# Two fixed expert pairs loaded ahead, the router by token, and the shared expert in turns 2 and 8

## Chip, cores and metric

The kernel runs on one core of a Trainium2 chip. The metric is device time in microseconds (us) of one launch, as the median of several runs. The granted TensorE clock of a row is a share of full speed: 1.00 is 2.4 GHz, 0.50 is 1.2 GHz.

## The reference

256 tokens of width 1024 go through two transformer blocks. The first block ends in a mixture of experts, and that is where the change lies:

```
h2 = modulate(rms_norm(x, norm2_g), shift2, scale2)
y  = moe_ffn(h2, w_router, router_bias, w_gate_e, w_up_e, w_down_e, w_gate_sh, w_up_sh, w_down_sh)
x  = rms_norm(x + gate2 * y, final_g)

def moe_ffn(xt, ...):                      # xt: 256 tokens x 1024
    scores = sigmoid(xt @ w_router)        # 64 experts
    choice = scores + router_bias          # best groups of 8, then the 8 best experts of a token
    wts    = scores of the 8 chosen, normed to a sum of 2.5
    routed = sum over chosen experts of swiglu(xt, gate_e, up_e, down_e) * wts
    return routed + swiglu(xt, w_gate_sh, w_up_sh, w_down_sh)

swiglu(x, g, u, d) = (silu(x @ g) * (x @ u)) @ d      # inner width 256
```

The second block begins with a gated feed-forward part (FF1, inner width 2816), whose first norm uses `ffn1_pre_g_2`. Attention and a second feed-forward part follow. All data are fp32.

## The kernel before

The program is written engine by engine, with semaphores between the engines. Each engine works off its own instructions in the order in which they stand. SP issues nearly all loads, also in order: a wait in SP's queue holds back every load behind it.

Dense products are kept exact by splitting both operands into a high and a low part (fp32r) and doing three matmuls. ACT makes the high parts (`split_hi`, `transposed`), DVE the low parts (`split_lo`), TensorE (`pe`) multiplies. Expert products are plain fp32 matmuls on the raw weights.

The weights of the dense parts live in `raw_g`, `raw_d`, `g_hi`, `g_lo`, `d_hi` and `d_lo`. The expert stage lays its `ring` over the same memory: two slots, each for one pair of experts (gate, up and down of both, six transfers of 1024 KB).

**Routing.** After the second output projection (groups `G_WO`, `G_WO+1`) DVE writes the normed rows to `h` and counts `h_ready`. Then TensorE transposes `h` for all 256 tokens, ACT and DVE split the transposed rows and the router's weights, and TensorE computes scores with experts on partitions (L2557, L2560). They are turned back and DVE picks the experts of each token in `route(b)` (L1672 to L1693), b being the block of 128 tokens. TensorE then counts the rows of each expert and ranks them (L2572 to L2579), DVE sets small and big flags (L1700 to L1705), TensorE sums them up (L2586 to L2589), and DVE computes the place of each expert in the order of turns (L1713 to L1723). TensorE applies the places (L2593 to L2595), and DVE writes `order_i` (L1733), on which SP waits (`ordered`) to load experts by their place.

The shared expert is one step of the dense machinery (`G_SH`, `D_SH`). Its gate/up stands on TensorE between the scores and the ranks, its down part on both sides of the last routing step.

**Turns.** 64 experts are worked off in 28 turns, `KINDS = "PPQPPBPPQPPPBPPQPPBPPPPBPPPQ"`. P is a plain turn of two experts with up to 64 rows each, Q a quad turn of four experts with up to 32 rows (it takes two pairs, so both slots of the ring), B one big and one small expert. Each turn consists of: gate/up of its rows (`rows_gate_up`, L2178), a gather of the rows of a later turn by matmuls with 0/1 matrices (`fill`, L2155; `pick_rows` makes the matrices), the addition of the last turn's result to the tokens' sums (`scatter`, L2215), the row weights (`pick_t`, L2167), the turn of the product (L2188) and the down part (`rows_down`, L2203). A pair's gate and up transfers wait for the gate/up of the turn that had the slot (`used_gu`), its down transfers for that turn's down part (`y_ps`). The first gather needs the tokens split in `tok` (ACT L906, DVE L1728), four fills, and their copies to `xg`. If an expert has more rows than its place takes, a slow path (`over`) runs afterwards.

Only turn 0's pair is fixed before: experts 0 and 1, in places 0 and 1. Its gate and up are loaded once the shared gate/up's low parts exist. The second pair waits for `ordered` and for the end of the shared expert.

```
            sp.wait_ge(M.used_g, 2 * G_SH + 2)
            sp.wait_ge(M.used_d, D_SH + 2)
            sp.wait_ge(ordered, 1)
            for _, places, load, _, _ in TURNS[1:]:
```

After the last turn SP loads FF1's first weights (L492), then the tables of the neighbourhood attention (L648), then FF1's further weights.

Of the kernel before, what the change touches and what calls it, by code (L numbers as in the profile page):

```python
# [59 lines left out]
G_SH = G_WO + 2  # L60
G_FF1 = G_SH + 1
# [5 lines left out]
D_SH, D_FF1, D_FF2 = 0, 1, 1 + N_FF  # L67
# [3 lines left out]
FIRST_SMALL, FIRST_BIG, N_SMALL = 2, 60, 20  # L71
# [10 lines left out]
def turn_table():  # L82
# [4 lines left out]
    for i, kind in enumerate(KINDS):  # L87
# [4 lines left out]
        elif kind == "B":  # L92
            places = (FIRST_BIG + both, FIRST_SMALL + 4 * quads + both)
            both += 1
            parts = [(0, 0), (0, 32), (0, 64), (1, 0)]
        else:
            places = (plain, plain + 1) if i else (0, 1)
            plain += 2 if i else 0
            parts = [(0, 0), (1, 0)]
# [16 lines left out]
TURN_OF = [t for t, (_, places, _, _, _) in enumerate(TURNS) for _ in range(len(places) // 2)]  # L116

# [6 lines left out]
def build(nc, a, out):  # L124
    ctx = ExitStack()
    with ctx:
# [28 lines left out]
        zeros = sb("zeros", [P, 512], BF16)  # L155
        over_i = sb("over_i", [1, 4], mybir.dt.int32)
# [17 lines left out]
        mod_rows, c_bc = lay(at_end - 4 * 4 * T, at_end, F32, ("mod_rows", [P, 512]), ("c_bc", [P, DC, 32]))  # L174
        ring, = lay(ring_at, ring_end, F32, ("ring", [P, 2, 6 * UNIT]))
# [53 lines left out]
        score_t = rt[0:E, 12 * E:16 * E]  # L229
# [3 lines left out]
        w_rt_hl = [t[:, :, :].rearrange("p c t -> p (c t)").rearrange("p (c e) -> p c e", c=DC) for t in (at_hi, at_lo)]  # L233

        final_g, pre1, post1 = area(36, D), area(40, D), area(44, D)
# [93 lines left out]
        class Stream:  # L329
# [3 lines left out]
            def __init__(self, tag):  # L333
# [13 lines left out]
                                           "tb", "nb", "mods", "g2r", "t1", "n1", "tw", "nw", "wrt", "rbias", "gains",  # L347
# [53 lines left out]
        for g in [*range(G_WIN, G_WIN + N_WIN), W_SMALL, W_Q, G_MLA, W_K, W_V]:  # L401
# [19 lines left out]
        def cols(m):  # L421
# [2289 lines left out]
```

## Time and profile before

| | us |
|---|---|
| median of 3 runs | 1341.66 (1339.59 to 1341.88) |
| the profiled execution, its own time | 1339.06 |
| its span in the trace | 1336.1 |
| busy: PE | 1217.5 (91%) |
| busy: DVE | 553.5 (41%) |
| busy: ACT | 451.6 (34%) |
| DMA moved | 359.51 MB, mean 269 GB/s |

The profiled execution's own time is 2.96 above its span: what lies around it. "Busy" counts an engine's instructions; a busy PE may run at either level of its clock. The 40 slices of the page are 33.4 us each, so the routing lies in slice 8 and 9 and the turns in slices 10 to 23.

### The profile page before, as it was taken

The page shows a single profiled execution, that of the slowest core. Times are in us where ns is not written, and L with a number is a line of the kernel's source. Part 1 is how long each engine was busy: PE and PEld are TensorE (multiplying, and loading weights), DVE is VectorE, ACT ScalarE, POOL GpSimd, SP SyncE. Part 2 cuts the span into 40 slices and gives each one's busy share as a digit, 9 for nine tenths or more (in the row PEclk, how much of TensorE's full clock was granted, in tenths as well). Part 3 has the DMA queues.
Part 4 walks back from the last instruction along what each step waited for, and adds up shares of the span by engine and source line. Part 5 has one row for each costly group of instructions (what it writes and reads, how often), then busy time and mean ns, then how long its engine had stood idle before and what let it go on. Part 6 is the DMA issues. An engine that isn't in the chain of part 4 may idle for free.

```text
span 1336.1 us, 16400 instructions
## 1 busy us (share of the span) xinstructions
PE 1217.5 (91%) x6541; PEld 844.7 (63%) x6544; DVE 553.5 (41%) x815; ACT 451.6 (34%) x656; POOL 45.7 (3%) x66
## 2 busy tenths in 40 slices
PE   5999998799899599889999769999989987899998
PEld 2877777674355244434444337888879866788886
DVE  1555546673022111112211155554456645544444
ACT  1345445341022111112212134333345544433333
POOL 0000000000000000000000020210010001000000
PEclk8899999899899899989999879999999978899999
DMA  9996655459999999999999996465615106355540
GB/s 370 351 365 223 233 202 165 182 205 412 387 422 420 393 422 420 421 391 421 421 421 420 421 283 193 167 203 187 231 57 190 63 1 221 132 198 186 186 146 31
DMA packets 115170, 359.51 MB, mean 269 GB/s; under 512 B 15077, under 2 KB 62614, under 8 KB 84063
## 3 DMA queue, kind: packets, MB, share of 16 engines
q1 hardware_dynamic: 113376, 352.71, 69.8%
q0 software_dynamic: 320, 3.46, 0.6%
q10 hardware_dynamic: 1406, 2.42, 0.5%
q8 instruction: 46, 0.75, 0.2%
q14 instruction: 22, 0.17, 0.0%
HBM read 355.37 MB, written 4.50 MB: 269 GB/s over the span
## 4 chain that ended last, share of the span: by engine, by line
PE 82%; DMA 8%; DVE 5%; ACT 3%; issue 1%; SPq 1%; POOL 1%; DVEq 0%; POOLq 0%; ACTq 0%
PE bank L1965 30%; PE bank L2178 16%; PE bank L2105 9%; DMA ring<-in_w_up_e 6%; PE bank L2203 5%; PE bank L2052 4%; PE bank L2155 3%; PE bank L2215 3%; PE bank L1981 1%; PE bank L2270 1%; PE bank L2292 1%; DMA arena<-in_w_ada 1%; PE bank L2021 1%; SPq L588 1%; PE bank L2094 1%
## 5 line engine op out<-in xcount | busy, mean ns | idle before, releaser
L2178 PE MATMUL bank<-ring,xg 128*64 128x512 f32 (+1 forms) x1152 | 212.8, 638 | 40.8 <-DMA ring<-in_w_up_e 40.8
L1965 PE MATMUL bank<-g_hi,xt_hi 128*128 128x512 f32 (+1 forms) x592 | 239.9, 405 | 5.8 <-DVE xt_lo L1881 2.2
L1256 DVE TENSOR_TENSOR g_lo<-raw_g,g_hi 128x2048 fp32r<-128x2048 f32 (+2 forms) x86 | 197.2, 2295 | 114.5 <-ACT g_hi L804 57.8
L1965 PE MATMUL bank<-g_hi,xt_lo 128*128 128x512 f32 (+1 forms) x592 | 232.7, 393 | 0.0
L1965 PE MATMUL bank<-g_lo,xt_hi 128*128 128x512 f32 (+1 forms) x592 | 232.1, 392 | 0.0
L2178 PEld LDWEIGHTS bank<-ring,xg 128*64 128x64 f32 (+1 forms) x1152 | 66.1, 133 | 184.1 <-issue 184.0
L1965 PEld LDWEIGHTS bank<-g_hi,xt_hi 128*128 128x128 f32 x592 | 112.9, 191 | 35.6 <-issue 10.2
L1965 PEld LDWEIGHTS bank<-g_hi,xt_lo 128*128 128x128 f32 x592 | 112.4, 190 | 24.1
L1965 PEld LDWEIGHTS bank<-g_lo,xt_hi 128*128 128x128 f32 x592 | 112.9, 191 | 21.2
L804 ACT ACTIVATE g_hi<-raw_g 128x2048 fp32r<-128x2048 f32 (+3 forms) x42 | 78.2, 1865 | 78.3 <-PE bank L1965 40.1
L1401 DVE SCALAR_TENSOR_TENSOR arena<-arena,w_row_of,bank 128x256 f32<-128x256 f32 x28 | 13.4, 480 | 218.4 <-ACT arena L924 214.3
L2203 PE MATMUL bank<-ring,a_t 128*64 128x512 f32 (+1 forms) x576 | 102.2, 597 | 1.4 <-DVE pickT L1359 0.9
L802 ACT ACTIVATE g_hi<-raw_g 128x2048 fp32r<-128x2048 f32 x46 | 87.9, 1912 | 18.6 <-PE bank L1965 16.9
L924 ACT ACTIVATE arena<-bank 128x256 f32<-128x256 f32 x28 | 10.8, 385 | 237.2 <-PE bank L2178 237.2
L1391 DVE TENSOR_TENSOR y_lo<-bank,y_hi 128x512 fp32r<-128x512 f32 x56 | 38.7, 692 | 102.8 <-ACT y_hi L917 102.8
L1276 DVE TENSOR_TENSOR d_lo<-raw_d,d_hi 128x2048 fp32r<-128x2048 f32 x21 | 50.7, 2417 | 45.7 <-ACT d_hi L848 45.7
L2105 PE MATMUL bank<-d_hi,at_hi 128*128 128x512 f32 x168 | 65.8, 392 | 0.4 <-DVE at_lo L1292 0.4
L2105 PE MATMUL bank<-d_hi,at_lo 128*128 128x512 f32 x168 | 65.4, 390 | 0.0
L2105 PE MATMUL bank<-d_lo,at_hi 128*128 128x512 f32 x168 | 65.4, 389 | 0.0
L2203 PEld LDWEIGHTS bank<-ring,a_t 128*64 128x64 f32 (+1 forms) x576 | 30.3, 124 | 52.6 <-issue 48.3
L848 ACT ACTIVATE d_hi<-raw_d 128x2048 fp32r<-128x2048 f32 x21 | 40.3, 1917 | 53.1 <-PE bank L2105 52.5
L917 ACT ACTIVATE y_hi<-bank 128x512 fp32r<-128x512 f32 x56 | 33.4, 597 | 70.1 <-PE bank L2203 70.1
(364 smaller groups left out, 1613.0 us busy)
## 6 DMA issues: line engine op xcount, KB each, us to landing
ring<-in_w_gate_e SPq DMA_DIRECT2D x64, 1024.0 KB, 12.3
ring<-in_w_up_e SPq DMA_DIRECT2D x64, 1024.0 KB, 16.4
ring<-in_w_down_e SPq DMA_DIRECT2D x64, 1024.0 KB, 15.6
raw_g<-in_ffn_w_gu SPq DMA_DIRECT2D x44, 1024.0 KB, 8.3
raw_g<-in_w_in SPq DMA_DIRECT2D x26, 1024.0 KB, 7.5
raw_d<-in_ffn_w_down SPq DMA_DIRECT2D x22, 1024.0 KB, 5.0
ada_d<-in_w_ada SPq DMA_DIRECT2D x16, 1024.0 KB, 6.7
raw_g<-in_w_out SPq DMA_DIRECT2D x8, 1024.0 KB, 5.3
```

The lines of the kernel that those rows point to most:

```text
L802: act.activation(dst, raw_gated(g, u), ACT.Copy).then_inc(S.hi_g, 1)
L804: act.activation(g_hi[:, u, 0:cols], raw_dense(g, u)[:, 0:cols], ACT.Copy).then_inc(S.hi_g, 1)
L848: act.activation(d_hi[:, :], raw_d[:, d % 2, :], ACT.Copy).then_inc(S.hi_d, 1)
L1256: dve.tensor_tensor(lo, raw, hi.bitcast(F32), ALU.subtract).then_inc(S.lo_g, 1)
L1276: dve.tensor_tensor(d_lo[:, :], raw_d[:, d % 2, :], d_hi[:, :].bitcast(F32), ALU.subtract)\
L1965: last = pe.matmul(out_, src[s][:, c, b * P:(b + 1) * P], w((g_hi, g_lo)[m], i), start=start and i == 0 and k == 0, stop=stop and i == len ...
L2052: last = pe.matmul(bank(banks[m // 2])[:, (m % 2) * T:(m % 2 + 1) * T], (g_hi, g_lo)[w][:, u, c * 512 + m * P:c * 512 + (m + 1) * P], (xt_ ...
L2105: last = pe.matmul(bank(2 * b + m), a_hl[i][:, c, b * P:(b + 1) * P], d_hl[w][:, c * D + m * 512:c * D + (m + 1) * 512], start=False, stop ...
L2155: last = pe.matmul(fill_bank(n)[:, i * 4 * ROWS:(i + 1) * 4 * ROWS], tok[k][:, b, c, :], pick[:, q % 2, b, :], start=k == 0 and b == 0 and ...
L2178: last = pe.matmul(bank(4)[r, :].rearrange("p (g n) -> p g n", g=2), xg[:, s // 2 % 2, c, at_:at_ + r.stop - r.start], gate_up_raw(pair, j ...
L2203: last = pe.matmul(bank(5 + m)[r, :], a_t[:, c, r], down_raw(pair, j, c, m), start=c == 0, stop=c == 1, skip_group_check=True)
L2215: last = pe.matmul(bank(2 * b + m), pickT[:, s % 2, b * P:(b + 1) * P], t[:, m * 512:(m + 1) * 512], start=False, stop=s == N_TURN - 1 and ...
```

## The change

- The first four places are fixed: experts 63 and 62 for turn 0, 61 and 60 for turn 1 (`FIRST_SMALL` 2 to 4). SP loads both pairs ahead of the order: the first once the low parts of `G_WO+1` exist, the second once TensorE has used them. Their gather matrices come from `pick_first`, without the order.
- The router works by token: TensorE transposes a block, ACT copies it to `tok_t` unsplit, and eight plain fp32 matmuls give the scores with tokens on partitions. The tokens are split in contiguous copies, and the fills read them with a step of 8 elements.
- The shared expert leaves the routing and the dense machinery. It is done in plain fp32 in two halves of its inner width: gate/up of half 0 ahead of turn 2's gate/up, its turn and down part ahead of turn 3's; the same for half 1 at turns 8 and 9. Its weights go to memory of their own (`g_sh`, `d_sh`).
- `pick_t(0)` moves behind turn 0's gate/up; the first four fills go to banks 5 and 6 and are copied by ACT alone.
- Gain rows: `final_g` is loaded behind the early pairs, `pre1` ahead of FF1's first weights, the other three behind the neighbourhood tables.
- The scratch memory of GpSimd's transfers is made smaller.

```diff
-FIRST_SMALL, FIRST_BIG, N_SMALL = 2, 60, 20
+FIRST_SMALL, FIRST_BIG, N_SMALL = 4, 60, 20
+SH_TURNS = (2, 8)
...
-            gated_stream(M, G_SH, D_SH, 1, lambda s, it: (a["w_gate_sh"][0], a["w_up_sh"][0]),
-                         lambda s, it: a["w_down_sh"][0])
-            for dst, n in ((final_g, "final_g"), (pre1, "ffn1_pre_g_2"), (post1, "ffn1_post_g_2"),
-                           (mixpre, "mix_pre_g_2"), (mixpost, "mix_post_g_2")):
-                src = a[n].rearrange("(o n) -> o n", o=1) if n == "final_g" else a[n]
-                sp.dma_start(dst, src.to_broadcast([P, D])).then_inc(in_["gains"], 16)
-            sp.wait_ge(M.lo_g, 2 * G_SH + 2)
-            load_gate_up(0, (0, 1))
-            sp.wait_ge(M.lo_d, D_SH + 1)
-            load_pair_down(0, (0, 1))
-            sp.wait_ge(M.used_g, 2 * G_SH + 2)
-            sp.wait_ge(M.used_d, D_SH + 2)
+            for k, n in enumerate(("w_gate_sh", "w_up_sh")):
+                sp.dma_start(g_sh[:, k, :, :], a[n][0].rearrange("(p c) n -> p c n", c=DC)).then_inc(sh_in, 16)
+            sp.wait_ge(M.lo_g, 2 * (G_WO + 1) + 2)
+            load_gate_up(0, (E - 1, E - 2))
+            load_pair_down(0, (E - 1, E - 2))
+            sp.wait_ge(M.used_g, 2 * (G_WO + 1) + 2)
+            load_gate_up(1, (E - 3, E - 4))
+            load_pair_down(1, (E - 3, E - 4))
+            sp.wait_ge(in_["mods"], 512)
+            for k in range(2):
+                sp.dma_start(d_sh[k], a["w_down_sh"][0][k * P:(k + 1) * P, :]).then_inc(sh_in, 16)
+            sp.dma_start(final_g, ...).then_inc(in_["gains"], 16)
             sp.wait_ge(ordered, 1)
-            for _, places, load, _, _ in TURNS[1:]:
+            for _, places, load, _, _ in TURNS[2:]:
...
             sp.wait_ge(used_gu, 4 * N_TURN)
+            sp.dma_start(pre1, a["ffn1_pre_g_2"].to_broadcast([P, D])).then_inc(in_["gains"], 16)
...
+            tok_high(0)
+            tok_turned(0)
+            tok_turned(1)
+            tok_high(1)
+            scores(0)
+            tok_turned(2)
+            tok_turned(3)
+            scores(1)
...
+                dve.wait_ge(rt_sc, b + 1)
                 link(dve.tensor_tensor(ch, sc, rbias, ALU.add))
...
             route(1).then_inc(rt_sel, 1)
-            lo_down(D_SH)
-            gate(M, 0, 0)
+            tok_rest(1)
...
-                gathered(1)
-                gathered(3)
+                pick_rows(1)
                 row_weight(0)
-                pick_rows(1)
                 rows_beyond()
                 rows_of_big()
...
-                                last = pe.matmul(fill_bank(n)[...], tok[k][:, b, c, :],
+                                last = pe.matmul(fill_bank(n)[...], tok[k][:, b, c:D:DC],
...
+            def sh_chunks(k, b, cs):
+                for c in cs:
+                    last = pe.matmul(sh_bank(b).rearrange("p (g n) -> p g n", g=2), tok_t[:, c, b * P:(b + 1) * P],
+                                     g_sh[:, :, c, k * P:(k + 1) * P], start=c == 0, stop=c == DC - 1)
+            def sh_turn(k):
+                pe.wait_ge(sh_dve, 2 * k + 2)
+                for b in range(TB):
+                    last = pe.transpose(bank(7)[:, b * P:(b + 1) * P], a_sh[b], ident)
+            def sh_down(k):
+                pe.wait_ge(sh_act, SH_PE[k])
+                for b in range(TB):
+                    for m in range(2):
+                        pe.matmul(bank(2 * b + m), sh_t[:, b, :], d_sh[k][:, m * 512:(m + 1) * 512], ...)
...
+                    if s == SH_TURNS[0]:
+                        pe.wait_ge(sh_in, 64)
+                        sh_gate_up(0, 0)
+                        sh_gate_up(0, 1)
+                        pe.wait_ge(sh_dve, 2)
+                    if s == SH_TURNS[1]:
+                        sh_gate_up(1, 0)
+                        sh_gate_up(1, 1)
+                        pe.wait_ge(sh_dve, 4)
+                    if s - 1 in SH_TURNS:
+                        pe.wait_ge(xg_sb, 2 * s)
+                        sh_turn(SH_TURNS.index(s - 1))
+                        sh_down(SH_TURNS.index(s - 1))
                     rows_gate_up(s)
+                    if s == 0:
+                        pick_t(0)
...
-            transposes(2)
+            for b in range(TB):
+                transposes(2, qs=(2 * b, 2 * b + 1))
+                for u in range(2):
+                    pe.wait_ge(M.xt_hi, 8 + 2 * b + u + 1)
+                    for c in range(4 * u, 4 * u + 4):
+                        last = pe.matmul(score_bank(b), tok_t[:, c, b * P:(b + 1) * P], w_rt[:, c, :],
+                                         start=c == 0, stop=c == DC - 1)
+                last.then_inc(rt_ps, 1)
...
-            gate_up(M, G_SH, 0, 0)
-            gate_up(M, G_SH, 0, 1)
             pe.wait_ge(rt_sel, 1)
...
-            down(M, D_SH, 0)
-            pe.wait_ge(rt_sel, 3)
-            down(M, D_SH, 1)
...
-    nc = bacc.Bacc("TRN2", target_bir_lowering=False, num_devices=1)
+    nc = bacc.Bacc("TRN2", target_bir_lowering=False, num_devices=1, dynamic_dma_scratch_size=4096)
```

## Rows read from the trace of the kernel before

Times are us from the span's start. A timeline row is: start, duration, engine, line, operation, tiles and shapes, count, and in brackets the idle time before it and what ended it.

**Rows 1.** The page: DMA busy, in tenths, in 40 slices

```profile
DMA  9996655459999999999999996465615106355540
```

**Rows 2.** Windows: busy time and count by engine, PEclk, DMA share, GB/s

```profile
262.00:263.00 1.00, 0.00 (x0) 0.00 (x0) 1.00 (x1) 0.57 (x1) 1.00 (x1) 0.50 0.00 0
452.00:454.00 2.00, 2.00 (x18) 1.21 (x10) 0.48 (x1) 0.39 (x1) 0.00 (x0) 1.00 0.19 78
600.00:700.00 100.00, 100.00 (x583) 49.22 (x585) 20.74 (x57) 21.13 (x40) 0.00 (x0) 1.00 1.01 421
```

**Rows 3.** The chain: start us, us, engine, tile, line

```profile
274.93 11.11 PE bank L1965 x48
286.03 0.17 PE bank L2572 x2
...
288.15 0.28 PE bank L2586 x4
...
289.15 0.38 ACT by_expert L903
...
297.11 4.10 PE bank L2155 x32
...
302.59 7.02 PE bank L2178 x32
...
336.15 9.79 PE bank L2178 x64
...
358.45 8.78 PE bank L2178 x32
...
375.42 6.87 PE bank L2178 x32
...
390.52 7.00 PE bank L2178 x64
...
444.39 8.58 PE bank L2178 x64
```

**Rows 4.** Timeline of SP's queue, 290 to 350

```profile
297.75 0.88 SPq L588 DMA_DIRECT2D ring<-in_w_gate_e  x2
...
323.30 0.85 SPq L588 DMA_DIRECT2D ring<-in_w_gate_e  x2
...
346.11 0.86 SPq L588 DMA_DIRECT2D ring<-in_w_gate_e  x2
```

**Rows 5.** Timeline of DVE, the router and turn 0

```profile
274.96 0.23 DVE L1672 TENSOR_TENSOR arena<-bank,arena 128x64 f32<-128x64 f32 x1 [1.16 <-PE bank L2566]
...
282.92 0.26 DVE L1693 TENSOR_SCALAR arena<-arena 128x64 f32<-128x64 f32 x1
...
302.63 0.33 DVE L1357 COPY w_row_of<-bank 64x1 f32<-64x1 f32 x2 [0.70 <-PE bank L2167]
...
305.82 0.32 DVE L1368 TENSOR_SCALAR row_big<-row_of 128x8 f32<-128x8 f32 x3
```

**Rows 6.** Timeline of PE, 229 to 266

```profile
230.04 1.16 PE L1952 MATMUL bank<-con,h_tok 128*128 128x128 f32 x8 [2.58 <-DVE h_tok L1615]
...
263.07 1.97 PE L1952 MATMUL bank<-con,h_tok 128*128 128x128 f32 x8 [6.26 <-DVE h_tok L1650]
```

**Rows 7.** Timelines of ACT, 257 to 292 and 775 to 790

```profile
258.30 1.06 ACT L814 ACTIVATE h_tok<-x_res 128x1024 f32<-128x1024 f32 x1 [9.84 <-DVE x_res L1644]
...
289.43 4.29 ACT L906 ACTIVATE xt_hi<-h_tok 128x1024 fp32r<-128x1024 f32 x2
...
781.51 3.71 ACT L802 ACTIVATE g_hi<-raw_g 128x2048 fp32r<-128x2048 f32 x2 [1.66 <-DMA raw_g<-in_ffn_w_gu]
```

**Rows 8.** An issue of SP, and landing times of two gain rows

```profile
241.56 0.49 SPq L618 DMA_DIRECT2D arena<-in_mix_post_g  x1
...
arena<-in_final_g SPq DMA_DIRECT2D x1, 512.0 KB, 9.8
...
arena<-in_mix_post_g SPq DMA_DIRECT2D x1, 512.0 KB, 14.4
```

More of the change, by code:

```diff
@@ L59 @@
 G_WO = G_WB + 2
-G_SH = G_WO + 2
-G_FF1 = G_SH + 1
+G_FF1 = G_WO + 2
 G_WIN2 = G_FF1 + N_FF
@@ L96, in turn_table @@
         else:
-            places = (plain, plain + 1) if i else (0, 1)
-            plain += 2 if i else 0
+            places = (plain, plain + 1) if i >= FIRST_SMALL // 2 else (2 * i, 2 * i + 1)
+            plain += 2 if i >= FIRST_SMALL // 2 else 0
             parts = [(0, 0), (1, 0)]
@@ L155, in build @@
         zeros = sb("zeros", [P, 512], BF16)
+        tok_t = sb("tok_t", [P, DC, T])
+        sh_t = sb("sh_t", [P, TB, P])
+        final_g = sb("final_row", [P, D])[:, :]
         over_i = sb("over_i", [1, 4], mybir.dt.int32)
@@ L228, in build @@
         past_cap, w_past = rt[:, 2 * E:4 * E], rt[:, 4 * E:6 * E]
-        score_t = rt[0:E, 12 * E:16 * E]
         w_over = area(34, TB * E).rearrange("p (b e) -> p b e", b=TB)
         rbias = area(35, E)
-        w_rt_hl = [t[:, :, :].rearrange("p c t -> p (c t)").rearrange("p (c e) -> p c e", c=DC) for t in (at_hi, at_lo)]
-        final_g, pre1, post1 = area(36, D), area(40, D), area(44, D)
+        g_sh = area(40, 2 * UNIT).rearrange("p (g c n) -> p g c n", g=2, c=DC)
+        d_sh = (area(36, D), d_sh1[:, :])
+        a_sh, silu_sh = ([t[:, 1, b * P:(b + 1) * P] for b in range(TB)] for t in (a_sb, silu))
+        pre1, post1 = area(40, D), area(44, D)
         mixpre, mixpost = area(48, D), area(52, D)
@@ L1115, in _, with tok_high, tok_turned, scores @@
                 square_rows(1, b, x[:, b, :])
[L1116 to L1125 removed]
+            def tok_high(b):
+                act.wait_ge(h_ready, 4 + b + 1)
+                act.activation(tok[0][:, b, :], h[:, b, :], ACT.Copy).then_inc(tok_hi, 1)
+            def tok_turned(q):
+                act.wait_ge(M.xt_ps, 8 + q + 1)
+                act.activation(quarter(tok_t, q), quarter_bank(0, q), ACT.Copy).then_inc(M.xt_hi, 1)
+            def scores(b):
+                act.wait_ge(rt_ps, b + 1)
+                act.activation(score(b), score_bank(b), ACT.Sigmoid).then_inc(rt_sc, 1)
+            act.wait_ge(M.used_g, 2 * (G_WO + 1) + 2)
+            tok_high(0)
[6 more added lines that the diff above has]
+            scores(1)
             sparse_phase()
@@ L2247, in body @@
                     rows_down(s)
-                pe.wait_ge(tok_lo, 1)
-                pe.wait_ge(rt_sc, 3)
+                pe.wait_ge(M.xt_lo, 12)
                 for n in range(4):
                     fill(n)
-                pe.wait_ge(xg_first, 4)
-                pick_t(0)
+                pe.wait_ge(rt_sel, 3)
+                pe.matmul(bank(7)[0:1, P:P + E], od[low, 1:2], place[low, low], start=True, stop=True)
+                pe.matmul(bank(7)[:, 0:P], by_expert[:, 0:P], place[:, :], start=True, stop=True)
+                pe.wait_ge(xg_first, 3)
+                pe.matmul(bank(5)[:, 0:P], by_expert[:, P:2 * P], place[:, :], start=True, stop=True).then_inc(rt_pos, 1)
                 for s in range(N_TURN):
```

196 lines of the change are left out of this document (100 added, 96 removed).

## Prediction

> **What bounds the kernel now.** I read the page's busy slices first, then windows over the expert stage, then the chain, SP's queue and the engines' timelines around the router. The slices show DMA at 9 tenths for slices 10 to 22, where the expert weights come in, and 0 to 6 tenths around them [rows 1]. In the windows, DMA is full at 421 GB/s over 600 to 700 us [rows 2]. A pair of experts is six transfers of 1,048,576 bytes, so 14.95 us at that rate. TensorE needs 15.10 us for a plain turn (375.42 to 390.52) [rows 3]; a quad turn takes it as long, but brings two pairs. So the stage runs at the rate of the bytes, and DMA stands still only where a quad turn has emptied the ring of two pairs: share 0.19 at 452 to 454, right behind turn 8's gate/up [rows 2, 3]; the same holds behind turn 2's, when pair 4 is issued only at 346.11 [rows 4]. Its length hangs on when that stream starts and on those gaps.
>
> When it starts is set by routing. Pair 1 is issued only at 297.75, after the order is known and the shared expert's last use is over [rows 4]; the stream into the ring is steady from there. In the new kernel pairs 0 and 1 are fixed and need nothing from the router. They are 12 transfers, 30 us at 421 GB/s, allowed from about 250 and 257, so they lie complete before 285, and the stream of the other 30 pairs starts when turn 0's gate/up matmuls end. Call the end of turn n's gate/up Xn. Before: X0 = 302.59 + 7.02 = 309.6, X1 = 323.2 (the issue at 323.30), X2 = 346.0 (346.11), X8 = 444.39 + 8.58 = 453.0 [rows 3, 4]. After the two first loads are ahead, every later start follows X0, then X1 and X2.
>
> **Routing, up to X0.** The first transposes of the normed rows start at 263.07 and take 1.97 [rows 6]; nothing ahead of them changes on their path. Each block of tokens is now scored by itself. Eight fp32 matmuls of 64 columns: one of the rank matmuls of that size takes 0.17 at full clock [rows 3], I take 0.2; here the granted clock is 0.50, the 1.2 GHz level, after TensorE's hole from 257 (262 to 263 [rows 2]), and the same eight transposes take 1.97 against 1.16 at full clock [rows 6]. So 1.6 to 3.4 us, I take 2.6, with 0.3 for the sigmoid of block 0: route(0) starts at 268.0 instead of 274.96. Both routes took 274.96 to 283.18, 8.2 us [rows 5]; with 0.4 for block 1's later scores they end at 276.6. TensorE then is free, while before it was busy with the shared gate/up (11.11 us from 274.93) until 286.03 [rows 3]. Ranks and DVE's step behind them took 286.03 to 288.15, 2.1, with two more matmuls; now 1.7 at full, 2.8 at half clock, I take 2.2: 278.8. The next batch took 288.15 to 289.15, 1.0 to 2.0, I take 1.4: 280.2. The fixed pairs' picks (0.9 of DVE) lie beside it, and the fills need no place in the order: they start at once, while DVE's chain to the places, some 3 us, lies beside them. Splitting the tokens is also off the path: a contiguous 1024-column copy costs 1.06 like the squares, where the strided one cost 4.29 for two [rows 7], and it runs beside scores and routes.
>
> Fills: 4.10 [rows 3] at full clock, up to 8.2 at half. TensorE is nearly idle for 4 us before, and after such a gap turn 2 took 9.79 against 7.00 [rows 3]. I charge 1.5: 285.8. Last copy 0.8, then turn 0's gate/up 7.02: X0 = 293.6, 16.0 us earlier. With all ends at their best X0 is 290, at their worst (turn 0 itself partly at half clock) 300.
>
> **Turn 0 gets longer.** pick_t(0) now stands behind the gate/up, so DVE does row_weight(0), rows_beyond and rows_of_big after X0, which it did under those matmuls before. 302.63 to 306.14 less 0.9 for pick_rows is 2.6, after 0.45 for pick_t [rows 5]; the gate waits behind them, and fill(5) is no longer under ACT's copy. I make it 2.4 us before turn 1. X1 = 293.6 + 13.6 + 2.4 = 309.6; left: 13.6. Bounds 0 (if the order of the queues hid it) and 3.5.
>
> **The shared expert in turns 2 and 8.** Its price comes from turn rows: 16 fp32 matmuls of 512 columns and half width take 7.02, and 32 of quarter width take 7.00 [rows 3], so parts run side by side and full width costs 0.88 for 512 columns. One job's gate/up is 16 matmuls of 256 columns, 7.0 us; silu and product 0.7; then in the next turn two transposes and a copy 0.8, four matmuls of 512 columns 3.5, together 4.3. Turn 2: before, X2 - X1 = 22.8. Now TensorE has the rest of turn 1 (8.2, as from 375.42 + 6.87 to 390.52, and 0.3 for the flag), 7.7 for the job and a quad gate/up at full clock 7.0, since the 4.4 us hole that halved the clock is filled: 23.2. Costs 0.4: left 13.2. Turn 3: 8.2 + 4.3 = 12.5 against 12.4 from X2 to 358.45 [rows 3]; its gate/up then loses no clock, but DMA has work until X2 + 30, so neither counts. Turn 8: TensorE is ready at X2 + 12.5 + 7.0 + 4 x 15.1 + 8.2 + 7.7 = X2 + 95.8, the data at X2 + 98.4 (444.39 less 346.0). So the job is hidden, with 2.6 us to spare, and the shorter hole gives the gate/up back its clock: 7.0 for 8.58. DMA stands at X8, so 1.6 is gained: 14.8. Without that cover a job costs 7.7. Turn 9's part: 12.5 against 13.6, hidden.
>
> **Moved loads.** Five gain rows came at 239 to 242, in an idle DMA. final_g now goes with the early loads, hidden by routing. pre1 goes ahead of the first FF1 weights. The first landed 9.8 us after its issue and the fifth 14.4 after its own, four issues of about 0.5 us later, so 512 KB cost some (14.4 + 2.2 - 9.8) / 4 = 1.7 us [rows 8]. ACT waits for those weights until 781.51, splits them for 3.71 and only then squares for the norm that FF1 needs [rows 7]: 1.7 lost, 0 to 2.2. Left 13.1. The other three stand behind the neighbourhood tables, before the third FF1 tile: 5.1 us of DMA and 1.4 of SP; TensorE wants that tile some 6 us after ACT takes it, so 0. The small scratch affects only gpsimd's transfers, which land over 25 us before they are wanted: 0. The overflow path stays unused: by the reference's routing experts 60 to 63 get 27, 19, 11 and 13 rows, under the 64 of a fixed place, and four experts exceed 64.
>
> **Sum.** 16.0 - 2.4 - 0.4 + 1.6 - 1.7 = 13.1. The profiled execution took 1339.06, its span 1336.1; that gives a span of 1323.0 and 1326.0. The runs' median lies 2.6 above the profiled one: 1328.6.
>
> **Strides in the fills.** The fills now read their stationary tokens 8 elements apart (`c:D:DC`), 8 per fill, 16 per turn. The transposes of the normed rows load with the same step, and eight take 1.16 at full clock, some 0.12 each, the pace of the contiguous fills (32 in 4.10 is 0.13) [rows 3, 6]. So no cost. The Trainium skill, SBUF — State Buffer (note on SBUF "cachelines"), says otherwise: lines are 16 bytes, so fp32 may step 4 elements for free and each new line beyond pays. By it each load would be dearer than the sum has it; ACT's strided token copy, 2.14 against 1.06, agrees, the transposes don't.
>
> **Rivals.**
> (a) *Strided loads bind, slower* (8%). If a load doubles like ACT's copy, by 0.09 us, a turn grows 1.5 to 16.6 and TensorE outruns no pair's 14.95. First fills and turns 0, 1: 6 us; turn 8: 6 x 1.5 - 2 = 7; turn 15: 4.4; the eleven turns to 27: 15. Total 32, so about 1361. It costs all 13 at 0.05 us a load. Against it: the 1.16.
> (b) *Cold routing* (17%). Bursts never lift the clock and fills and turn 0 run at half for long: X0 near 299, about 1334.
> (c) *The job costs double* (5%), at half clock or unpaired: 7 at turn 2, 4.4 at turn 8 and the 1.6: no gain, 1341.
> (d) *The change doesn't do what it says* (4%): the fixed pairs land late, behind a wait ahead of them in SP's queue. Pair 1's gate/up landing only at 316 would leave X1 as it was: 1341. Against: 30 us of transfers in 35.
> (e) *Better than forecast* (10%): turn 0's 2.4, the fills' 1.5 and FF1's 1.7 hidden: 1323.
>
> **Numbers.** My forecast has the other 56%, with 1325 to 1332 for itself. Range 1323 to 1336. No change is within 0.2% (2.7 us), about what a measurement can tell: 5% (half of c and d, which are spread round it); slower 10% (a and 2 of c and d); faster 85% (the rest).
>
> **What would show it.** After: routes end near 276 to 278; gate transfer of the third pair issued at 292 to 296; 16 us from there to the next; no hole before turn 2, one under 3 us before turn 8, its gate/up at clock 1.00; fills at 0.13 a matmul; the expert stage's last gate/up some 15 us earlier, FF1's first split 1.7 later after it. Wrong if a turn is over 15.5, if DMA stands still in plain turns, or if the fixed pairs land after 287.

## The result and the profile after

The changed kernel takes 1368.22 us (median of 4 runs, 1366.64 to 1371.48), the one before 1340.62 on the same chip (4 runs, 1339.05 to 1341.88). The ratio is 1.021, 95% interval 1.0185 to 1.0235: slower by 27.6 us, where 13 faster was forecast. The profiled execution has a span of 1365.0 (before 1336.1).

The page of the changed kernel: busy time by engine, and DMA's busy tenths in slices of 34.1 us. Answer to [rows 1]:

```profile
PE 1271.7 (93%) x6551; PEld 899.9 (66%) x6554; DVE 540.8 (40%) x810; ACT 444.3 (33%) x657; POOL 44.2 (3%) x66
...
DMA  9996755766998899899999899555535205365540
```

TensorE is busy for 54 us more, and the row of nines of [rows 1] has eights in it: the same bytes now wait for TensorE. Where the 54 us lie is told by the groups of instructions by line and shape. The fills have two such groups of matmuls, one for the high and one for the low part of the tokens: they grow by 27.4 and 27.5 us. First the changed kernel, then the one before (busy us, mean ns of one):

```profile
L2227 PE MATMUL bank<-pick,xt_hi 128*128 128x256 f32 x224 | 77.2, 427 | 0.2 <-DVE over_i L1452 0.2
L2227 PEld LDWEIGHTS bank<-pick,xt_lo 128*128 128x128 f32 x224 | 64.9, 338 | 0.0
```

```profile
L2155 PE MATMUL bank<-pick,xt_hi 128*128 128x256 f32 x224 | 49.8, 304 | 1.2 <-DVE xt_lo L1728 1.0 <-DVE over_i L1398 0.2
L2155 PEld LDWEIGHTS bank<-pick,xt_lo 128*128 128x128 f32 x224 | 34.6, 190 | 0.0
```

These are the same fills, with the same shapes and the same count; a weight load of them takes 338 ns instead of 190. The chain of the changed kernel, answer to [rows 3], shows what that does to a turn:

```profile
263.27 1.94 PE bank L1996 x8
265.22 3.51 PE bank L2648 x16
...
282.62 7.57 PE bank L2227 x32
...
291.02 7.02 PE bank L2252 x32
...
309.44 6.87 PE bank L2252 x32
...
326.87 7.12 PE bank L2190 x32
...
335.03 7.07 PE bank L2252 x64
...
374.11 6.87 PE bank L2252 x32
380.98 2.13 PE bank L2227 x8
...
385.60 1.92 PE bank L2227 x8
...
391.11 7.00 PE bank L2252 x64
...
566.38 10.77 DMA ring<-in_w_up_e
...
587.97 10.98 DMA ring<-in_w_up_e
```

From 374.11 to 391.11 a plain turn has 17.00 us, and over four turns the mean is 17.07 (X3 364.0 to X7 432.3), where before it had 15.10 [rows 3]; gate/up and down are unchanged, the two fills of 8 matmuls grew from 1.15 and 0.95 to 2.13 and 1.92. A pair's transfers take 14.95. So TensorE is the bound of the turns. From turn 0 to turn 14 the chain holds no transfer, where before it had one in front of turns 2, 3, 8 and 9. It still enters DMA around the quad turns 15 and 27 (566.38, 587.97 and 778.36), where TensorE waits for the two pairs of a quad turn or for the pair behind it. SP's queue agrees; answer to [rows 4]:

```profile
250.41 0.80 SPq L600 DMA_DIRECT2D ring<-in_w_gate_e  x2
...
256.95 0.81 SPq L600 DMA_DIRECT2D ring<-in_w_gate_e  x2
...
298.27 0.88 SPq L600 DMA_DIRECT2D ring<-in_w_gate_e  x2
...
381.19 0.86 SPq L600 DMA_DIRECT2D ring<-in_w_gate_e  x2
...
398.40 0.85 SPq L600 DMA_DIRECT2D ring<-in_w_gate_e  x2
```

The fixed pairs come early, as meant. The stream then begins at 298.27 instead of 309.8, and in plain turns the next pair is asked for some 17.1 us after the last (17.2 from 381.19 to 398.40).

Below, the ends of gate/up Xn are compared in one table, so that each stretch can be seen by itself. It is made from the chains: start and duration of the gate/up rows, added. "Contiguous" is the changed kernel with contiguous fills, the first experiment; "all edits" is the ninth. The forecast's column is worked out from the terms of the prediction.

| | before | forecast | after | contiguous | all edits |
|---|---|---|---|---|---|
| first transposes | 263.1 | 263.1 | 263.3 | 262.4 | 263.1 |
| X0 | 309.6 | 293.6 | 298.0 | 295.9 | 294.0 |
| X1 | 323.2 | 309.6 | 316.3 | 313.1 | 308.0 |
| X2 | 346.0 | 332.8 | 342.1 | 337.0 | 331.9 |
| X8 | 453.0 | 438.2 | 457.6 | 444.3 | 437.6 |
| X15 | 575.4 | 560.6 | 586.0 | 567.3 | 561.0 |
| X27 | 772.9 | 758.1 | 799.6 | 765.3 | 759.1 |
| span | 1336.1 | 1323.0 | 1365.0 | 1331.8 | 1322.4 |

### The profile page after: what moved, and what is told of

The parts are those of the page before. It is cut to its first block, busy times and chain, and to the rows that moved or that the text cites. A ratio compares the mean times of both kernels' runs of the same rounds, so it can differ in the third digit from the quotient of the medians.

```text
span 1365.0 us, 16392 instructions
## 1 busy us (share of the span) xinstructions
PE 1271.7 (93%) x6551; PEld 899.9 (66%) x6554; DVE 540.8 (40%) x810; ACT 444.3 (33%) x657; POOL 44.2 (3%) x66
## 4 chain that ended last, share of the span: by engine, by line
PE 86%; DVE 4%; DMA 4%; ACT 3%; issue 1%; POOL 1%; SPq 0%; DVEq 0%; POOLq 0%; ACTq 0%
PE bank L2009 29%; PE bank L2252 15%; PE bank L2149 9%; PE bank L2227 8%; PE bank L2277 6%; PE bank L2096 4%; PE bank L2289 3%; DMA ring<-in_w_up_e 2%; PE bank L2025 1%; PE bank L2361 1%; PE bank L2383 1%; DMA arena<-in_w_ada 1%; PE bank L2190 1%; PE bank L2065 1%; PE bank L1996 1%
## 5 line engine op out<-in xcount | busy, mean ns | idle before, releaser
L2009 PE MATMUL bank<-g_hi,xt_hi 128*128 128x512 f32 (+1 forms) x576 | 234.1, 406 | 5.7 <-DVE xt_lo L1925 2.2
L1296 DVE TENSOR_TENSOR g_lo<-raw_g,g_hi 128x2048 fp32r<-128x2048 f32 (+2 forms) x84 | 192.7, 2295 | 116.2 <-ACT g_hi L817 58.4
L2009 PE MATMUL bank<-g_hi,xt_lo 128*128 128x512 f32 (+1 forms) x576 | 226.9, 394 | 0.0
L2009 PE MATMUL bank<-g_lo,xt_hi 128*128 128x512 f32 (+1 forms) x576 | 226.1, 393 | 0.0
L2252 PE MATMUL bank<-ring,xg 128*64 128x512 f32 (+1 forms) x1152 | 202.1, 610 | 13.1 <-DMA ring<-in_w_up_e 11.0
L2009 PEld LDWEIGHTS bank<-g_hi,xt_lo 128*128 128x128 f32 x576 | 109.6, 190 | 23.5
L1455 DVE SCALAR_TENSOR_TENSOR arena<-arena,w_row_of,bank 128x256 f32<-128x256 f32 x28 | 13.5, 481 | 185.9 <-ACT arena L950 185.9
L2227 PE MATMUL bank<-pick,xt_hi 128*128 128x256 f32 x224 | 77.2, 427 | 0.2 <-DVE over_i L1452 0.2
L2227 PEld LDWEIGHTS bank<-pick,xt_hi 128*128 128x128 f32 x224 | 63.5, 332 | 20.0 <-issue 19.7
L2227 PE MATMUL bank<-pick,xt_lo 128*128 128x256 f32 x224 | 72.4, 405 | 0.0
L929 ACT ACTIVATE xg<-bank 128x512 f32<-128x512 f32 x56 | 33.5, 597 | 99.1 <-PE bank L2227 99.1
L2227 PEld LDWEIGHTS bank<-pick,xt_lo 128*128 128x128 f32 x224 | 64.9, 338 | 0.0
```

Source lines behind the costliest of these rows:

```text
L1296: dve.tensor_tensor(lo, raw, hi.bitcast(F32), ALU.subtract).then_inc(S.lo_g, 1)
L2009: last = pe.matmul(out_, src[s][:, c, b * P:(b + 1) * P], w((g_hi, g_lo)[m], i), start=start and i == 0 and k == 0, stop=stop and i == len ...
L2227: last = pe.matmul(fill_bank(n)[:, i * 4 * ROWS:(i + 1) * 4 * ROWS], tok[k][:, b, c:D:DC], pick[:, q % 2, b, :], start=k == 0 and b == 0 a ...
L2252: last = pe.matmul(bank(4)[r, :].rearrange("p (g n) -> p g n", g=2), xg[:, s // 2 % 2, c, at_:at_ + r.stop - r.start], gate_up_raw(pair, j ...
```

## The experiments

Theory A is the prediction's rival (a): strided weight loads make TensorE the bound. The rivals are given with each run. Unless said otherwise a kernel computes the whole reference.

**1. Contiguous fills in the changed kernel.** The tokens are split into chunks by strided copies, as before the change, and the fills read them with a step of 1:

```diff
-act.activation(tok[0][:, b, :], h[:, b, :], ACT.Copy).then_inc(tok_hi, 1)
+act.activation(tok[0][:, b, :, :], h_chunks[:, b, :, :], ACT.Copy).then_inc(tok_hi, 1)
...
-last = pe.matmul(fill_bank(n)[...], tok[k][:, b, c:D:DC],
+last = pe.matmul(fill_bank(n)[...], tok[k][:, b, c, :],
```

> The changed kernel, but the split tokens are written chunk by chunk, as before the change, so that the fills read their stationary operand with step 1; all else stays. Theory A (the step of 8 makes each weight load dearer, the turns grow from 15.1 to 17.06 us and TensorE becomes the bound): the fills return to 0.12 to 0.13 us a matmul, plain turns to 15.1, the DMA share of the stage to 1.00, and the time to 1329 to 1337, 1333 most likely, since X0 came 4.4 later than forecast. The strided copies on ACT delay the scores by about 1. Theory B (the turns grow from something else: the shared expert's reads, other banks, the early pairs): the turns stay near 17 and the time above 1355.

Measured: 1334.32 us, ratio to before 0.997 (0.9949 to 0.9991). The step of the fills is worth 32 us by the ratios (1.021 against 0.997) and 34 by X27 (799.6 against 765.3). The turn is back at 15.1 to 15.2 (X4 372.6, X5 387.8, X6 403.0), and a load of the fills takes 197 ns instead of 338:

```profile
L2229 PEld LDWEIGHTS bank<-pick,xt_lo 128*128 128x128 f32 x224 | 36.0, 197 | 0.0
```

But only 4 of the forecast's 13 us appear: something else is short of the forecast by 9.

**2. Only the step.** The kernel before, with contiguous token copies and fills at a step of 8, nothing else of the change.

> The kernel before, with one part of the change alone: tokens split in contiguous copies and fills reading them with step 8. Theory A: turns of 17.0 us, 27 of them times 1.93 us less some 8 of slack ahead of the quad turns, less 2 for the shorter copies: about 42 slower, 1383. Theory B: 1339 to 1341, as before.

Measured: 1370.96 us, ratio 1.0224 (1.0198 to 1.0251): 30 us slower by the ratio, 32 by the medians. The step alone makes the whole loss, without early pairs, router or shared expert. Its turn is 17.1 too (X4 387.8, X5 404.9). The 42 us that I expected were too many.

**3. No shared expert.** The kernel of the first experiment with `SH_TURNS = (-5, -9)`: the shared expert's product is left out, its weights are still loaded.

> As e1_contiguous, but the shared expert is left out of the computation altogether. The forecast's step (0.4 lost at turn 2, 1.6 won at turn 8 through the clock): within 2 us of e1_contiguous, rather slower than faster. Rival (the job is not covered at turn 2, since TensorE is ready for turn 2 only 4 to 5 us after its data): 3 to 6 us faster than e1_contiguous. A job that costs its whole length twice would give 15 to 20 faster.

Measured: 1335.26 us, ratio 0.9974 (0.9955 to 0.9994), the same as with the shared expert. X2 - X1 falls from 23.9 to 22.7, which is the 22.8 of before, but the time does not follow: TensorE's hole at turn 8 is then longer (6.5 us idle for 2.0) and its gate/up, part of it at half clock, takes 9.7 for 8.8. What the two jobs cost in their turns is made up at turn 8, and the "job costs double" rival falls.

**4. The load by itself.** A bench that computes nothing of the reference: rows of identical matmuls on one core, each row with another step of the weights or another kind of operand.

```diff
+for i in range(32):    # step 1, 2, 4, 8; fp32r, 256 columns moving
+    pe.matmul(banks[i % 2][:, 0:256], xr[:, 1, k:k + 127 * step + 1:step], xr[:, 0, 0:256], ...)
```

> Only a row of matmuls from tokens in SBUF, none of the computation: 32 of each kind after a warm-up. fp32r, 256 columns moving, stationary step 1, 2, 4, 8; step 8 with 512 moving; fp32 transposes with stationary step 1 and 8; fp32 matmuls of 64 columns with step 1 and 8; last a moving operand of step 4. Theory A: at fp32r step 8 costs 0.24 a matmul and step 1 0.12. If the cost comes from lines of 16 bytes, steps 1, 2 and 4 are alike at 0.12 and only 8 is dear; if from any step above 1, 2 and 4 are dear too. With 512 moving, 0.23 if the load runs beside the matmul ahead of it, 0.35 or more if not. The transposes: 0.12 at both steps, as the trace of before has it at step 8; if they are dear at 8 here, their row of before was misread.

The timeline of TensorE in the bench: L51 has step 1 with 512 columns moving, L53 has step 1, L55 step 2, L57 step 4, L59 step 8, L61 step 8 with 512 columns moving, L63 and L65 are fp32 transposes at step 1 and 8, L67 and L69 plain fp32 with 64 columns at step 1 and 8 (two records a matmul), and L71 has the weights at step 1 and its 256 moving columns at step 4. Then windows of five of the stretches: busy PE, PEld, ACT and POOL with their counts, granted clock, DMA share and GB/s.

```profile
7.75 16.14 PE L51 MATMUL b<-xr 128*128 128x512 f32 x64 [7.75 <-ACT xr L38]
23.73 4.00 PE L53 MATMUL b<-xr 128*128 128x256 f32 x32
27.56 4.00 PE L55 MATMUL b<-xr 128*128 128x256 f32 x32
31.40 7.64 PE L57 MATMUL b<-xr 128*128 128x256 f32 x32
38.87 7.87 PE L59 MATMUL b<-xr 128*128 128x256 f32 x32
46.58 8.13 PE L61 MATMUL b<-xr 128*128 128x512 f32 x32
54.55 3.65 PE L63 MATMUL b<-con,x 128*128 128x128 f32 x32
58.04 3.75 PE L65 MATMUL b<-con,x 128*128 128x128 f32 x32
61.63 7.26 PE L67 MATMUL b<-x 128*128 128x64 f32 x64
68.72 15.45 PE L69 MATMUL b<-x 128*128 128x64 f32 x64
83.94 7.85 PE L71 MATMUL b<-xr 128*128 128x256 f32 x32
```

```profile
12.00:16.00 4.00, 4.00 (x19) 3.33 (x18) 0.00 (x0) 0.00 (x0) 1.00 0.00 0
39.00:46.00 7.00, 7.00 (x31) 7.00 (x31) 0.00 (x0) 0.00 (x0) 1.00 0.00 0
58.50:61.00 2.50, 2.50 (x25) 2.50 (x24) 0.00 (x0) 0.00 (x0) 1.00 0.00 0
69.00:72.00 3.00, 3.00 (x14) 3.00 (x14) 0.00 (x0) 0.00 (x0) 1.00 0.00 0
89.50:91.00 1.50, 1.50 (x8) 1.34 (x7) 0.00 (x0) 0.00 (x0) 1.00 0.00 0
```

At full clock, with nothing beside it: 0.12 us a matmul at steps 1 and 2 (from one row's start to the next, over 32), 0.23 and 0.24 at steps 4 and 8. Behind 512 moving columns most of it is hidden: 0.25 at step 8 (L61) against 0.23 at step 1 (L51: 53 matmuls that start between 11.7 and 23.5). The fills move 256 columns, so their pace is that of the load. The transposes do not pay: 0.109 at step 1, 0.112 at step 8. That is the trap of the prediction in one line: its evidence, the 1.16 us of eight transposes, was right and said nothing about the fills.

Two more rows narrow down what the transposes have that the fills have not. It is not the plain fp32 type: at full clock (69 to 72) the 14 records of L69 start 0.24 apart, where those of L67 start 0.11 apart. And a step is not free on the moving side either: L71 runs at half clock at first, but its last 8 matmuls, at full clock (89.7 to 91.4), start 0.24 apart, twice the 0.12 of L53. A transpose moves 128 columns, half as many, so an estimate from L71 gives it 0.12 if the strided operand is the one that moves, which is the pace that it has anyway. Whether that is why the transposes do not pay was not shown: no run tells which operand they load as weights.

Of the two patterns that I had expected (1, 2 and 4 alike, or all above 1 dear) neither came: the price begins between 2 and 4.

The Trainium skill, SBUF — State Buffer (note on SBUF "cachelines"), gives the 16-byte line as the unit and asks for two hits on each for full rate. The bench agrees with that: two fp32 in 16 bytes at step 2 are free, one at step 4 is not. It does not agree with the same note's "4 fp32" as the free stride.

**5. pre1 in a hole.** From here on each kernel is that of the first experiment with one edit, to find the missing 9 us. Here `pre1` is loaded ahead of the pair that waits for turn 15's gate/up.

```diff
+PRE1_AT = 15
...
+if load >= 2 and TURN_OF[load - 2] == PRE1_AT and (load < 3 or TURN_OF[load - 3] != PRE1_AT):
+    sp.dma_start(pre1, a["ffn1_pre_g_2"].to_broadcast([P, D])).then_inc(in_["gains"], 16)
...
 sp.wait_ge(used_gu, 4 * N_TURN)
-sp.dma_start(pre1, a["ffn1_pre_g_2"].to_broadcast([P, D])).then_inc(in_["gains"], 16)
```

> The kernel with contiguous tokens, and pre1 loaded ahead of the pair that waits for turn 15's gate/up, instead of ahead of FF1's first weights. Theory A: pre1 ahead of FF1's weights is on the path; in the contiguous-token kernel the first weights are ready 11.5 us after the last gate/up (765.3 to 776.8), before the change 8.6 (772.9 to 781.5). So 2.9 us come back: 1334.3 becomes about 1331.4, and the hole at turn 15 hides the load. Rival B: the second half of the weights or ACT's queue sets FF1's start, and the time stays at 1334 +- 1. Rival C: inside the turns the load is not hidden, X27 moves 1.2 later and the gain is 1.7: 1332.6.

Measured: 1331.11 us, ratio 0.9925 (0.991 to 0.9939). The chains behind the last gate/up, without and with the edit:

```profile
766.36 10.45 DMA raw_g<-in_ffn_w_gu
776.88 3.71 ACT g_hi L819 x2
```

```profile
767.03 7.90 DMA raw_g<-in_ffn_w_gu
775.00 3.71 ACT g_hi L821 x2
```

From X27 to ACT's split it takes 8.7 us instead of 11.6, and X27 lies no later (its first transposes started 1.1 later, and so did X27): 2.9 us, as theory A had it, hidden in the hole.

**6. Row work later.** `rows_beyond` and `rows_of_big` move behind turn 0's gate and the next row weights on DVE.

```diff
 row_weight(0)
-rows_beyond()
-rows_of_big()
 for s in range(N_TURN):
     body(s)      # in body(0), behind row_weight(1):
+        rows_beyond()
+        rows_of_big()
```

> The kernel with contiguous tokens, with rows_beyond and rows_of_big behind turn 0's gate and row weights on DVE. Theory A: turn 0's extra time is DVE's queue: X1 - X0 was 17.24 there against 13.54 before the change, with TensorE idle from 297.9 to 299.7 for the gate and the clock at 0.60 right after. The gate comes some 1.6 us earlier and the clock stays up: X1 - X0 about 14.7 and the median 1332 (2.4 less). Rival B: the gate waits for row_weight(0), which itself waits for pick_t(0): then under 1 us, 1333.7.

Measured: 1330.43 us, ratio 0.9931 (0.9906 to 0.9957), an interval that overlaps a little with that of the first experiment. X1 - X0 is 13.9, where it was 17.2 without the edit and 13.5 before the change. The transposes of turn 0's product, without and with the edit:

```profile
299.73 0.70 PE L2264 MATMUL bank<-con,arena 128*128 128x128 f32 x2 [1.82 <-DVE arena L1457]
300.09 0.78 PE L2229 MATMUL bank<-pick,xt_hi 128*128 128x256 f32 x2
```

```profile
297.18 0.46 PE L2265 MATMUL bank<-con,arena 128*128 128x128 f32 x2
297.59 0.50 PE L2230 MATMUL bank<-pick,xt_hi 128*128 128x256 f32 x2
```

The 1.82 us of idle are gone, and with them the half clock behind (granted 0.60 over 300 to 304 without the edit, 1.00 over 296 to 300 with it). The wait was 1.8, its price 3.3.

**7. Turned copies first.** ACT does `tok_turned(0)`, `tok_turned(1)` ahead of `tok_high(0)`, and the same for block 1.

> The kernel with contiguous tokens, ACT's turned copies ahead of its token copies. Theory A: the token copy of block 0 (2.15 us) holds the first turned copy back from 263.4 to 264.4, so the scores start 1.0 us earlier and X0 with them: 1333.3. Rival B: block 1's scores are bound by TensorE, which is freed 1 us earlier too, or by something behind (DVE's token rest, 2.0 us): no change, 1334.3.

Measured: 1335.14 us, ratio 0.9947 (0.993 to 0.9964); the interval overlaps that of the first experiment, so the time does not tell. The trace does: the scores start 1.83 us after the transposes instead of 2.63, and X0 lies 33.0 after them instead of 33.5. The 0.8 is there, half of it arrives.

**8. TensorE kept busy.** Matmuls of zeros stand where TensorE had nothing to do.

```diff
+busy(24)          # bf16, 512 columns, ahead of transposes(2)
...
+busy(12)          # ahead of the ranks
 zero_sums().then_inc(M.used_d, 1)
```

> The kernel with contiguous tokens, and 24 matmuls of zeros (bf16, 512 columns) in TensorE's hole ahead of the normed rows' transposes, 12 more ahead of the ranks. Theory A: the low clock (0.50 from 262 to 286) is what made X0 later than forecast. With the clock up, transposes and scores of both blocks take about 7 us for 11.5, ranks and next batch 2.4 for 4.2, the fills 4.1 for 5.4: X0 about 289 to 290 instead of 295.9, and the median 1327 to 1329. Rival B: DVE (two routes of 4.1 us each, one behind the other) and the pair-1 loads (complete at about 285) bound it, and X0 gains only 3: 1331. Rival C: the zeros delay the real work or don't hold the clock: 1334 or more.

Measured: 1331.09 us, ratio 0.9941 (0.9918 to 0.9964), an interval that overlaps that of the first experiment; and X0 lies 32.5 after the transposes, only 1.0 better. Scores of the two blocks, then windows (busy PE, PEld, DVE, ACT and POOL, granted clock, DMA share and GB/s):

```profile
264.19 3.34 PE L2655 MATMUL bank<-arena,tok_t 128*128 128x64 f32 x16 [1.53 <-ACT tok_t L1152]
...
269.07 3.67 PE L2655 MATMUL bank<-arena,tok_t 128*128 128x64 f32 x16
```

```profile
262.00:266.00 4.00, 2.47 (x16) 2.28 (x16) 3.96 (x3) 4.00 (x4) 0.00 (x0) 0.82 1.01 424
266.00:270.00 4.00, 4.00 (x21) 3.77 (x20) 2.29 (x18) 2.04 (x4) 0.00 (x0) 0.50 1.02 424
```

The zeros lift the clock for the transposes (1.16 for eight instead of 1.94), then TensorE waits 1.53 for ACT's copy and the clock falls within the scores. The time is the one of rival B, but its mechanism is not: what holds X0 is rival C's, zeros that do not hold the clock. My 6 us were wrong. Of the rest of the median's 3 us the trace has 1.6 at turn 8, whose gate/up keeps its clock; without and with the zeros:

```profile
435.45 8.77 PE L2254 MATMUL bank<-ring,xg 128*32 128x512 f32 x64 [2.03 <-DMA ring<-in_w_up_e]
```

```profile
433.71 7.07 PE L2258 MATMUL bank<-ring,xg 128*32 128x512 f32 x64 [1.67 <-DMA ring<-in_w_up_e]
```

The three kernels with zeros (this one, and two of experiments 9 to 11) have this 7.1, behind holes of 1.67, 1.70 and 1.99 us; the five without them (experiments 1, 5, 6, 7 and one of 9 to 11) have 8.8, behind 1.98 to 2.09. So the length of the hole alone does not decide; what else does is open, since the zeros stand 150 us ahead of it.

**9 to 11. All four edits; without the zeros; and tokens at a step of 2.** The last lays the tokens out as pairs of chunks, so that a fill reads every second element:

```diff
-tok = [....rearrange("p (b c n) -> p b c n", b=TB, c=DC)
+tok = [....rearrange("p (b c n e) -> p b c n e", b=TB, c=DC // 2, e=2)
...
-last = pe.matmul(..., tok[k][:, b, c, :],
+last = pe.matmul(..., tok[k][:, b, c // 2, :, c % 2],
```

> The kernel with contiguous tokens and all four edits together: pre1 loaded in turn 15's hole, the row work behind turn 0's gate, turned copies first, zeros on TensorE ahead of the transposes and the ranks. Theory A: the places are separate, so the gains seen in the traces add: 2.9 at FF1, 3.3 at turn 0, 0.8 and 1.0 of routing, 8.0 in all from a ratio of 0.997: about 0.991, so 1329 against 1341. Rival B: what turn 0 gives back is lost at turn 2, where the shared job holds TensorE while the data are there: 1332 or more.

> The same without the zeros. Theory A: the clock falls to 0.50 within the scores whatever stands ahead of them, and the zeros gave only 1.0 us, at the ranks and fills: 1.0 above the kernel with them. Rival B: the zeros also shift what comes later (the clock in a later stage) and the difference is over 2 us, either way.

> All four edits, and the tokens laid out so that the fills read with a step of 2 elements (8 bytes). Theory A: two elements lie in each 16 bytes, so the load keeps its pace (0.12 in the bench at a step of 2, 0.24 at 4 and 8): plain turn 15.1, the time that of the kernel with all four edits +- 1. Rival B: any step costs in this kernel, where the moving operand is read beside it: turn over 15.5, time over 1340.

Measured, against 1339.04 for the kernel before on the same chip:

| | us | ratio, 95% interval |
|---|---|---|
| all four edits | 1325.06 | 0.9897 (0.9883 to 0.9912) |
| without the zeros | 1327.80 | 0.9918 (0.9905 to 0.993) |
| all four, step of 2 | 1323.41 | 0.989 (0.9876 to 0.9905) |

The gains add: 0.9897 was expected as about 0.991. The zeros are worth 2.7 us here, more than the 1.0 I gave them, though the two intervals overlap a little; rival B of that run had it right. The traces have two parts. X0 lies 31.0 after the transposes with zeros and 33.0 without: with the turned copies first TensorE waits for 0.30 and 0.24 us, not the 1.53 of experiment 8, and the clock holds through both blocks (rows below). And from X0 to X8 it takes 143.6 against 145.2, which is turn 8's gate/up again (7.1 against 8.8).

```profile
264.51 2.00 PE L2658 MATMUL bank<-arena,tok_t 128*128 128x64 f32 x16 [0.30 <-ACT tok_t L1154]
266.35 1.10 PE L2001 MATMUL bank<-con,h_tok 128*128 128x128 f32 x8
267.69 2.00 PE L2658 MATMUL bank<-arena,tok_t 128*128 128x64 f32 x16 [0.24 <-ACT tok_t L1154]
```

The scores end 4.1 us earlier behind the transposes than without the zeros, and X0 only 2.0: DVE now goes from the first block's token rest through both routes without a gap, and TensorE sits idle for 4.06 ahead of the ranks. That is rival B of experiment 8, which holds only once the clock does.

At a step of 2 the fills keep their pace, 1.16 and 0.96 us for eight, and the turn its length (15.2 from X4 to X5). Its median lies 1.6 us below the contiguous one, with overlapping intervals; the trace has a reason for X0 (28.6 us after the transposes, against 31.0): the copies that write the tokens take 1.14 to 1.17 on ACT and 1.23 on DVE instead of 2.08 and 2.02, and DVE is earlier in its first route (its first `MAX8` at 267.6 against 269.2).

**12. Half the loads strided.** The kernel of the first experiment, with the low part of the tokens at a step of 8: 8 of a turn's 16 loads.

> The kernel with contiguous tokens, but the low part read with a step of 8, so 8 of the 16 loads of a turn. Theory A: each costs 0.12 more, TensorE's turn is 15.1 + 0.96 = 16.1, and it costs only where TensorE outlasts the transfers: first fills and turns 0, 1 about 3; turns 3 to 8 about 2; turns 9 to 15 none, since the quad turns wait for data with 6 us to spare; turns 16 to 27 about 4. Sum 9, so 1343. Rival B: a bank or port conflict that slows every turn in proportion, or the transfers: half of the 34 us between the two kernels, 1351. Rival C: no cost below some pace: 1334.

Measured: 1344.55 us, ratio 1.0043 (1.0031 to 1.0055), where 1343 was expected and 1351 by proportion. Within one turn the two kinds of load lie side by side (ns min/median/max):

```profile
L2230 PEld LDWEIGHTS bank<-pick,xt_hi x8: 187/191/210, 608.8 to 613.6; 128*128 128x128 f32 x8
...
L2230 PEld LDWEIGHTS bank<-pick,xt_lo x8: 312/328/340, 609.1 to 614.0; 128*128 128x128 f32 x8
```

The turn is 16.1 (X4 375.8, X5 391.9). Against the contiguous kernel X2 comes 1.8 later, of which the transposes' start explains 0.9; turns 3 to 8 2.3 (109.7 for 107.3), turns 9 to 15 nothing (122.9 for 123.0), turns 16 to 27 7.4 (205.3 for 198.0). So a longer turn costs only where TensorE outlasts the transfers: in the stretch to turn 15 the some 6 us more of TensorE are swallowed by the quad turn's wait for data. The last stretch has more than my 4, the first less than my 3. In the changed kernel, with twice as much on each turn, that wait did not cover it: turns 9 to 15 took 5.4 us more.

## Why the prediction was wrong

**The step that failed is "Strides in the fills": "The transposes of the normed rows load with the same step ... So no cost."** The transposes do run at 0.12 us with a step of 8 [rows 6], and the bench repeats it (0.112). But they are another operation, whose pace does not depend on the step, and the fills' loads are weights of a plain matmul, which at a step of 8 take 0.24 instead of 0.12 (bench, and 338 ns instead of 190 a load in the kernel). One other row was at hand with the right sign, ACT's strided copy at 2.14 against 1.06, and the rule of the Trainium skill (SBUF — State Buffer, note on SBUF "cachelines") stood beside it; the measured 0.24 at a step of 8 has the sign that this rule gives. I weighed the nearer-looking row and let it decide alone. Removing the step (experiment 1) takes away 34 us at X27, adding it alone to the kernel before (experiment 2) costs 30.

**A second reading made it look harmless.** "So the stage runs at the rate of the bytes" holds around the quad turns only. In the plain turns TensorE's 15.10 us already stood above the 14.95 of a pair, and the chain of the kernel before has no transfer in it from turn 4's gate/up to turn 7's (375.42 to 427.8). There was no slack for anything added: 1 us more of TensorE made the turn 16.1 (experiment 12), 2 us more 17.1.

**Rival (a) was right in mechanism and nearly in size.** It had 0.09 a load, a turn of 16.6 and a total of 32; measured were 0.12, 17.06 and 34.3 at X27. Its parts, after less contiguous in the table: to X2 5.1 (6), to X8 8.2 (7), to X15 5.4 (4.4), to X27 15.6 (15). I gave it 8%, where the evidence was one row against one row and a rule.

**The other terms, read with the step taken out.** They were to bring 13.1 and bring 4.3 (span 1331.8 against 1336.1). The figures are those of experiment 1, unless another is named.

- *Routing, 16.0.* X0 came 13.7 earlier, 13.0 of it behind the first transposes. Scores took 3.5 us a block at half clock for my 2.6, and the second block's stood behind the first on TensorE, so route(1) began at 274.3 and the routes ended at 278.4 for my 276.6. Ranks and next batch took 2.7 and 1.5 for my 2.2 and 1.4, the fills 5.4 for my 5.6. This is a piece of rival (b), cold routing: the clock stood at 0.50 from 262 to 286, as its rows say; X0 was 295.9, between the forecast and its 299.
- *Turn 0, -2.4.* It was -3.7. The queue on DVE was as told, but the idle 1.8 us also halved the clock for the 4 us behind it. Experiment 6 gives back 3.3.
- *Turn 2, -0.4.* X2 - X1 was 23.9 for my 23.2: -1.1. Data were there and TensorE was not, so the job held the turn; without it 22.7.
- *Turn 8, +1.6.* It did not come. The hole shrank to 2.0 us, the job lay hidden in it, but gate/up still took 8.8 at a clock of 0.57 (436 to 440). I had taken a smaller hole for no loss of clock; of the kernels of experiments 1 and 5 to 11 it was none only in the three with zeros (7.1), one of which had a hole of 1.99.
- *FF1, -1.7.* It was -2.9: 10.45 us for the first weights instead of 7.87. Another 0.4 is pre1's own issue on SP, which the term left out. It was also avoidable: experiment 5 hides the load.
- *Not in the sum.* These terms make 6.0. Another 1.4 goes between X2 and X27 (428.3 for 426.9 us), which no run here explains.

The early loads, the largest part, did what was said: both pairs on chip by 286 (in the changed kernel a DMA share of 0.92 over 282 to 286 and 0.02 over 286 to 290), the stream's start bound to X0 alone. Rivals (c) and (d) fall (experiment 3; SP's queue). And the forecast's 13 us exist: with four small edits, three of them at places that it named as losses, the kernel comes out at 0.9897 of before, 13.7 us faster in the profiled spans (1322.4 against 1336.1). That this is so near 13.1 is in part luck: X0 gains 15.6 of the 16.0 and turn 8 1.3 of the 1.6, but turn 0 loses 0.4 and not 2.4, FF1 0.3 and not 1.7, turn 2 1.1 and not 0.4, and another 1.6 goes between X8 and X27.

## What to carry to other kernels

Before a weight operand gets a stride, price the load in the very operation that will use it; a transpose or a copy with the same step is another price. Then ask which stretch has the slack: 1 us more a turn on TensorE was free over turns 9 to 15, where a quad turn waited for its data, and cost its full length in the plain turns 17 to 26 (16.1 for 15.1), where TensorE's time already stood above the 14.95 us of a pair. Where two layouts fight (cheap contiguous writes against strided reads), one in between may serve both: pairs of elements kept together read at full pace and were cheaper to write than the fully sorted ones.

A wait of 1.5 to 2 us on TensorE was worth more than itself three times here (turn 0, turn 8, the scores), because the clock was at 1.2 GHz behind it. It was not always so (holes of 1.67 to 1.99 at turn 8 in the kernels with zeros). Waits that short deserve a row in the sum, with bounds for both cases.

## What the runs showed of the hardware

- Weight loads of 128 columns fp32r: 0.12 us at steps of 1 and 2 elements, 0.23 at 4 and 0.24 at 8. So the price doubles between 2 and 4 and hardly grows from 4 to 8. Plain fp32 loads double too (0.11 to 0.24 a record at a step of 8).
- 256 moving columns fp32r at a step of 4 take 0.24 as well, with weights at a step of 1 (8 matmuls at full clock).
- 256 moving columns hide nothing of it (0.24 against 0.12), 512 most of it (0.25 against 0.23): in these rows the slower of load and stream sets the pace.
- fp32 transposes of a strided operand keep their pace (0.11 us). Which of their two operands is loaded as weights, and why the stride is free, no run here shows.
- Matmuls of zeros ahead of the transposes had these at full clock, but behind a wait of 1.53 us it fell again, where behind waits of 0.30 and 0.24 it did not. At turn 8 a hole of 1.98 was followed by the low clock in one kernel and one of 1.99 by the full clock in another.
